# The last gate chunk of a pooling mixer by seven block products too, and five low parts of weights on VectorE

## The chip, the cores and the metric

The kernel runs on one core of a Trainium2 chip. Its metric is the time of one execution on the device in microseconds (us), lower is better. The engines are TensorE (PE in the profile), VectorE (DVE), ScalarE (ACT), GpSimd (POOL) and SyncE (SP, which here issues nearly all the DMAs). Each runs its own instructions strictly in order; they meet only through semaphores.

## What is computed

Two blocks follow each other on a 1024 x 1024 float32 activation. The change touches the first one, and there the part from the input projection to the pooling branch's output projection:

```python
def first_block(x, ...):
    u = rms_norm(h, norm_in_g[l])
    proj = jnp.einsum('bsd,de->bse', u, w_in[l])              # 1024 -> 4096
    pool_x, pool_z, m_x, m_z = jnp.split(proj, [D_POOL, 2 * D_POOL, 2 * D_POOL + D_MLSTM], axis=-1)
    y_pool = pool_mixer(pool_x, pool_w[l], pool_scale[l]) * jax.nn.silu(pool_z)
    y_m = mlstm_branch(m_x, ...) * jax.nn.silu(m_z)
    h = h + jnp.einsum('bse,ed->bsd', jnp.concatenate([y_pool, y_m], axis=-1), w_out[l])

def pool_mixer(u, pool_w, pool_scale):
    ug = u.reshape(B, S, N_POOL_GROUPS, POOL_GROUP_DIM)       # 4 groups of 256
    pooled = stack([window_mean_minus_self(ug[:, :, g], w) for g, w in enumerate((2, 4, 8, 16))])
    mixed = jnp.einsum('bsgc,gcd->bsgd', pooled, pool_w).reshape(B, S, D_POOL)
    return mixed * pool_scale
```

`pool_z` (columns 1024 to 2047 of `w_in`, chunks 4 to 7) is the gate of the pooling branch.

## The kernel before

**Chunks.** Weights come in chunks of 1 MB, in the order of `chunk_plan` (line 90); chunk w of the plan is not the same as the column block c that stands in it. A chunk is loaded into the one buffer `wraw` by SP (`wt`), and split into a high part `whi` and a low part `wlo` (the raw value minus the high part), each in one of two buffers. A product of two float32 matrices is then three matmuls, low x high, high x low and high x high (`three`, lines 1064 to 1066), 128x512 each. In `group` TensorE makes one output tile of 128x512 of a chunk: 8 x 3 matmuls for `w_in`, four such groups in a chunk, or 4 x 3 matmuls for `w_out`, eight groups in a chunk.

**Seven products.** The chunks 2 to 8 of the plan (`SEVEN`, line 104) are computed another way: the chunk is cut into 2 x 2 blocks and the result made of seven block products in place of eight, each 4 x 3 matmuls (`seven`). Sums of blocks are made by GpSimd, their high parts by ScalarE (`cast_block`) and their low parts by VectorE and GpSimd (`low_block`). Each product's weights take one of eight slots, four in each side of `whi` and `wlo` (`place`, `slot`); VectorE adds the products up (`add_up`), and a finished chunk is stored to DRAM from `sz` (`store_7`), except the last, which is the gate of group 0 and stays in `sz`. Chunks 6 to 8 of the plan are gates of the pooling branch; the fourth gate is chunk 12, `W_SZ3`, by four plain groups.

**Behind the products** come, on TensorE: `W_POOL[1]` (chunk 9) with `mix(0)` between its second and third group, `W_POOL[2]` (10) and `mix(1)`, `W_POOL[3]` (11) and `mix(2)`, `W_SZ3` (12), and then `W_OP` (13 to 16), the output projection, with `mix(3)` after its fourth group. `mix(g)` is 4 x 6 matmuls, the pooled features of group g times `pool_w`. VectorE makes the pooled features in `window(g, m)`, their low parts in `low_mix(g)`, and in `mixed(g)` it takes the four results of `mix(g)` out, scales them by the gate `sz` into `yr`, waits for ScalarE's high part `yp_hi` (`high_y`), and makes the low part `yp_lo`. ScalarE's queue at group g is: four copies of a chunk's groups to `px` (`pooled`), `high_pw(g)`, which waits for the end of `mix(g - 1)`, `high_px(g, 0)`, `high_y` for the results of `mix(g - 1)`, `high_px(g, 1)`.

**Splitting a plain chunk.** `split` (line 798) on GpSimd waits for the chunk's load and for TensorE to be done with the chunk two before it, or, where that one went by products, with the last product on its side (`side_free`). It casts the high part (line 804) and, unless the chunk stands in `BY_VECTOR`, makes the low part (line 808). For a chunk in `BY_VECTOR` VectorE makes it in `low_w` (line 1796). TensorE waits for the low part before each group. SP loads chunk w only when `w_lo` has counted w low parts.

**Banks.** PSUM has eight banks of 128x512, named bank0 to bank3 and (as halves) wide0 and wide1. Products take them in turn; plain groups go round bank 0 to 3 (`ring_g`), mixes round the other four (`ring_x`). `take` makes TensorE wait until what a bank last held has been read.

## Time and profile before

| | |
|---|---|
| median of 3 runs | 1151.78 us (1151.3 to 1154.06) |
| profiled execution | 1151.01 us, its span 1149.2 us |
| TensorE busy | 1139.6 us (99%), 6515 matmul records |
| VectorE / ScalarE / GpSimd busy | 724.4 / 386.6 / 477.1 us |
| granted TensorE clock, mean | 0.999 |
| phase of products | about 62 to 196 us of the span |
| chunks 9 to 12 and the mixes | about 196 to 299 us |

Times in rows are in us from the span's start unless marked ns. Matmuls are pipelined: one lasts 0.39 us in the record, while the next starts 0.23 us after it, so the step from start to start tells the pace. "[2.60 <-DMA x]" behind a row is the idle time of the engine before it and what ended it.

### The profile page before, as it was taken

How to read it: one execution, taken by the hardware profiler on the slowest of the kernel's cores; microseconds unless marked ns; L12 is line 12 of the kernel's file. 1: busy time of each engine (PE TensorE's matmuls, PEld its weight loads, DVE VectorE, ACT ScalarE, POOL GpSimd, SP SyncE). 2: the span in 40 equal slices, each digit the busy share in tenths (PEclk: the TensorE clock that was granted, in tenths of full speed). 3: DMA queues.
4: the chain of work that ended last, by engine and by line, in shares of the span. 5: the costliest groups of instructions: out<-in, count | busy, mean ns of one | idle time of the engine just before them, and what ended most of it. 6: DMA issues, size and time to landing. Idle time of an engine off the chain costs nothing.

```text
span 1149.2 us, 17423 instructions
## 1 busy us (share of the span) xinstructions
PE 1139.6 (99%) x6515; PEld 930.8 (81%) x6515; DVE 724.4 (63%) x1336; ACT 386.6 (34%) x758; POOL 477.1 (42%) x474
## 2 busy tenths in 40 slices
PE   9999999999999999999999999999999999999997
PEld 6888888888888887788888888889888887777786
DVE  5944534567244894467777965884698434556668
ACT  7422233222100122546574621341111134553322
POOL 3356654422223231344666765304223224455534
PEclk9999999999999999999999999999999999999999
DMA  8323343222335522101114241232111220142113
GB/s 245 120 64 121 100 146 120 74 65 100 110 73 203 194 85 81 53 23 28 48 42 160 75 165 54 93 125 74 48 45 42 63 72 1 38 154 96 46 39 138
DMA packets 84229, 104.07 MB, mean 91 GB/s; under 512 B 14257, under 2 KB 61577, under 8 KB 82994
## 3 DMA queue, kind: packets, MB, share of 16 engines
q1 hardware_dynamic: 76422, 99.21, 26.0%
q10 hardware_dynamic: 7724, 3.74, 1.2%
q8 instruction: 53, 0.87, 0.3%
q14 instruction: 30, 0.25, 0.1%
HBM read 80.35 MB, written 24.17 MB: 91 GB/s over the span
## 4 chain that ended last, share of the span: by engine, by line
PE 96%; POOL 2%; issue 1%; DVE 1%; ACT 0%; ACTq 0%; POOLq 0%; DVEq 0%
PE bank L1064 22%; PE bank L1066 21%; PE bank L1065 21%; PE bank L1394 3%; PE bank L1369 3%; PE wide L1064 3%; PE wide L1065 3%; PE wide L1066 3%; PE wide L1594 2%; PE wide L1385 2%; PE bank L1333 1%; PE bank L1322 1%; PE bank L1569 1%; PE bank L1310 1%; PE bank L1106 1%
## 5 line engine op out<-in xcount | busy, mean ns | idle before, releaser
L804 POOL CAST whi<-wraw 128x2048 fp32r<-128x2048 f32 x24 | 48.1, 2003 | 336.8 <-PE bank L1066 267.7
L1064 PE MATMUL bank<-x_hi,wlo 128*128 128x512 f32 x312 | 123.5, 396 | 0.0
L1066 PE MATMUL bank<-x_hi,whi 128*128 128x512 f32 x312 | 121.6, 390 | 0.0
L1065 PE MATMUL bank<-x_lo,whi 128*128 128x512 f32 x312 | 121.5, 389 | 0.0
L1064 PE MATMUL bank<-u_hi,wlo 128*128 128x512 f32 x308 | 120.3, 391 | 0.0
L1066 PE MATMUL bank<-u_hi,whi 128*128 128x512 f32 x308 | 119.9, 389 | 0.0
L1065 PE MATMUL bank<-u_lo,whi 128*128 128x512 f32 x308 | 119.9, 389 | 0.0
L808 POOL TENSOR_TENSOR wlo<-wraw,whi 128x2048 fp32r<-128x2048 f32 x20 | 94.8, 4742 | 2.0 <-ACT whi L2909 0.5
L1064 PEld LDWEIGHTS bank<-x_hi,wlo 128*128 128x128 f32 x312 | 58.6, 188 | 16.2 <-issue 4.3
L1008 POOL TENSOR_SCALAR sp<-sp,rcx 128x384 f32<-128x384 f32 (+1 forms) x64 | 37.9, 606 | 76.4 <-DVE rcx L2393 76.3
L2306 DVE SCALAR_TENSOR_TENSOR wide<-glu,VT,wide 128x1024 f32<-128x1024 f32 x58 | 69.3, 1286 | 0.0
L1066 PEld LDWEIGHTS bank<-x_hi,whi 128*128 128x128 f32 x312 | 58.6, 188 | 12.4
L1064 PEld LDWEIGHTS bank<-u_hi,wlo 128*128 128x128 f32 x308 | 57.8, 188 | 13.1 <-issue 1.2
L1065 PEld LDWEIGHTS bank<-x_lo,whi 128*128 128x128 f32 x312 | 58.6, 188 | 11.7
L1066 PEld LDWEIGHTS bank<-u_hi,whi 128*128 128x128 f32 x308 | 57.8, 188 | 12.2
L1065 PEld LDWEIGHTS bank<-u_lo,whi 128*128 128x128 f32 x308 | 57.8, 188 | 11.8
L1394 PE MATMUL bank<-v,kwb 128*128 128x257 f32 x224 | 58.2, 382 | 0.2
L1369 PE MATMUL bank<-Cst,qT 128*128 128x257 f32 x224 | 58.0, 380 | 0.1
L932 POOL TENSOR_TENSOR Pm<-ST,Wb 128x128 f32<-128x128 f32 x64 | 30.0, 470 | 63.0 <-ACT Wb L2784 63.0
L1064 PE MATMUL bank<-whi,ym_lo 128*128 128x512 f32 x128 | 51.2, 400 | 0.0
L1066 PE MATMUL bank<-whi,ym_hi 128*128 128x512 f32 x128 | 49.9, 390 | 0.0
L1065 PE MATMUL bank<-wlo,ym_hi 128*128 128x512 f32 x128 | 49.8, 389 | 0.0
(431 smaller groups left out, 2840.9 us busy)
## 6 DMA issues: line engine op xcount, KB each, us to landing
wraw<-in_w_in SPq DMA_DIRECT2D x19, 1024.0 KB, 5.4
wraw<-in_w_out SPq DMA_DIRECT2D x12, 1024.0 KB, 5.4
wraw<-in_w_in SPq DMA_DIRECT2D x16, 512.0 KB, 4.8
xr<-in_x SPq DMA_DIRECT2D x8, 512.0 KB, 6.9
hst<-in_x SPq DMA_DIRECT2D x4, 1024.0 KB, 5.2
hpool<-hst SPq DMA_DIRECT2D x4, 1024.0 KB, 4.2
h<-hpool SPq DMA_DIRECT2D x4, 1024.0 KB, 7.0
resid<-h SPq DMA_DIRECT2D x8, 512.0 KB, 2.6
```

The costliest lines, as they stand in the source:

```text
L804: g_.tensor_copy(whi[w % 2][:, :, :], wraw[:, :, :]).then_inc(s["w_hi"], 1)
L808: g_.tensor_tensor(wlo[w % 2][:, :, :], wraw[:, :, :], whi[w % 2][:, :, :].bitcast(F32), ALU.subtract).then_inc(s["w_lo"], 1)
L932: g_.tensor_tensor(Pm[:, n % 2, :], STs[h % 2][:, ck, :], Wb[:, n % 2, :], ALU.mult).then_inc(s["g_P"], 1)
L1008: g_.tensor_scalar(row, row, rcx[:, x % 2, i:i + 1], 0.5 if g else 1.0, ALU.mult, ALU.mult).then_inc(s["g_nm"], 1)
L1064: pe.matmul(ps, al, bh, start=(k == 0), stop=False)
L1065: pe.matmul(ps, ah, bl, start=False, stop=False)
L1066: return pe.matmul(ps, ah, bh, start=False, stop=(k == nk - 1))
L1369: mm = pe.matmul(ps[:, 0:AUG], q[:, k, ck * P:(ck + 1) * P], Cst[:, d, k, :], start=(k == 0), stop=(k == 1))
L1385: pe.matmul(ps[:, 0:AUG], Pm[:, n % 2, :], v[:, ck, :], start=True, stop=True).then_inc(s["t_intra"], 1)
L1394: mm = pe.matmul(ps[:, 0:AUG], kwb[:, m % 2, k * P:(k + 1) * P], v[:, ck, :], start=True, stop=True)
L1594: mm = pe.matmul(ps[64 * i:64 * i + 64, 0:P], vt[:, lo + b, g * HD2:(g + 1) * HD2], pT_of(x, i)[:, b * P:(b + 1) * P], start=(b == 0), sto ...
L2306: ins = ve.scalar_tensor_tensor(dst, src, w, acc, ALU.mult, ALU.add)
```

## The change

Column block 7 of `w_in`, the fourth gate, moves from a plain chunk (`W_SZ3`, 12) into the products, which now are chunks 2 to 9 of the plan. `W_POOL[1]` to `W_POOL[3]` become chunks 10, 11 and 12; `W_OP` stays 13. With 56 products instead of 49 the two sides of the buffers come free in the other order, so behind the phase a chunk's buffer is `home(w)` and no longer w % 2. The gate in `sz` at the end of the phase is again that of group 0; the other three are stored and loaded back (`load_sz(1)` to `load_sz(3)`, one more than before). The low parts of the five chunks 10 to 14 are all made by VectorE (`W_POOL[1]` was already); GpSimd only casts there. The first four sums of the output projection are taken out before `mixed(3)`, and its groups all use banks 0 to 3. Where the diff changes `whi[w % 2]` to `whi[home(w)]` in other places, it is cut:

```diff
@@ -90,7 +90,7 @@
-    plan = [("w_in", c, "f") for c in (0, 12, 8, 9, 10, 13, 6, 5, 4, 1, 2, 3, 7)]
+    plan = [("w_in", c, "f") for c in (0, 12, 8, 9, 10, 13, 7, 6, 5, 4, 1, 2, 3)]
     plan += [("w_out_pool", c, "o") for c in (0, 2, 1, 3)]
@@ -101,7 +101,7 @@
-SEVEN = range(2, 9)
+SEVEN = range(2, 10)
@@ -112,12 +112,16 @@
-    W_POOL, W_SZ3, W_OP, W_MX, W_MZ, W_OM, W_2 = (0, 9, 10, 11), 12, 13, 14, 16, 20, 24
+    W_POOL, W_OP, W_MX, W_MZ, W_OM, W_2 = (0, 10, 11, 12), 13, 14, 16, 20, 24
     N7, S0 = len(SEVEN), SEVEN[0]
-    BY_VECTOR = (W_POOL[1], W_MZ + 2, W_MZ + 3, W_OM, W_OM + 1)
+    BY_VECTOR = (W_POOL[1], W_POOL[2], W_POOL[3], W_OP, W_OP + 1, W_MZ + 2, W_MZ + 3, W_OM, W_OM + 1)
     (W_BA, W_BB, W_AV, W_KV, W_Q0, W_AU, W_AG, W_CG0, W_BG, W_CG1, W_Q1) = range(W_2, W_2 + 11)
     W_O2 = W_2 + 11
+
+    def home(w):
+
+        return (w + (w > SEVEN[-1])) % 2
@@ -171,7 +175,7 @@
     um_d = nc.dram_tensor("umraw", [P, 6, S], F32).ap()
-    sz_d = nc.dram_tensor("szpool", [P, 2, 2, S], F32).ap()
+    sz_d = nc.dram_tensor("szpool", [P, 3, 2, S], F32).ap()
     row_t = nc.dram_tensor("relr", [8, RELS], F32)
@@ -375,7 +379,7 @@
         early = {
-            "l_sz": ("l_h0", 32), "l_um0": ("l_h1", 16), "l_um1": ("l_h2", 16), "l_um2": ("l_h3", 16),
+            "l_sz": ("l_h0", 48), "l_um0": ("l_h1", 16), "l_um1": ("l_h2", 16), "l_um2": ("l_h3", 16),
             "o_st0": ("l_kB", 16 * (N7 - 1)), "o_st1": ("l_ln", 16 * (N7 - 1)),
@@ -588,7 +592,7 @@
                 sp_.wait_ge(s["o_st1"], 16 * (N7 - 1))
-                sp_.dma_start(sz[:, :, :], sz_d[:, 2 - g, :, :]).then_inc(s["l_sz"], 16)
+                sp_.dma_start(sz[:, :, :], sz_d[:, 3 - g, :, :]).then_inc(s["l_sz"], 16)
@@ -613,9 +617,8 @@
             mix_weights(2)
-            wt(W_SZ3)
+            wt(W_OP)
             load_sz(2)
-            wt(W_OP)
             sp_.wait_ge(s["v_px"], 13)
@@ -639,6 +642,7 @@
                 load_h(0, q)
+            load_sz(3)
             wt(W_OP + 2)
@@ -798,14 +802,14 @@
                     if w - 2 in SEVEN:
-                        g_.wait_ge(s["t_prod"], side_free(w % 2))
+                        g_.wait_ge(s["t_prod"], side_free(home(w)))
                     elif w >= 2:
                         g_.wait_ge(s["t_gemm"], done(w - 2))
-                    g_.tensor_copy(whi[w % 2][:, :, :], wraw[:, :, :]).then_inc(s["w_hi"], 1)
+                    g_.tensor_copy(whi[home(w)][:, :, :], wraw[:, :, :]).then_inc(s["w_hi"], 1)
                 if w in BY_VECTOR:
                     return
                 g_.wait_ge(s["w_hi"], high_count(w))
-                g_.tensor_tensor(wlo[w % 2][:, :, :], wraw[:, :, :], whi[w % 2][:, :, :].bitcast(F32),
+                g_.tensor_tensor(wlo[home(w)][:, :, :], wraw[:, :, :], whi[home(w)][:, :, :].bitcast(F32),
                                  ALU.subtract).then_inc(s["w_lo"], 1)
@@ -1070,7 +1074,7 @@
                 _, _, layout = plan[w]
-                wh, wl = whi[w % 2], wlo[w % 2]
+                wh, wl = whi[home(w)], wlo[home(w)]
                 nk = KT
@@ -1242,8 +1246,6 @@
                 mix(g - 1)
-            for i in range(4):
-                group(W_SZ3, i, u_hi, u_lo, "a_sz", 8 + i + 1)
             pool_hi = lambda j: yp_hi[:, j, :]
@@ -1255,7 +1257,7 @@
                     group(W_OP + q, i, pool_hi, pool_lo, "v_hp", n,
-                          ps=ring_x("v_hp", n) if q == 0 and i >= 4 else None)
+                          ps=None)
@@ -1808,10 +1810,10 @@
-                if g in (1, 2):
+                if g:
                     ve.wait_ge(s["l_sz"], 16 * g)
                 else:
-                    ve.wait_ge(s["a_sz"], 8 + 4 * (g == 3))
+                    ve.wait_ge(s["a_sz"], 10)
                 for i in range(5):
@@ -1877,13 +1879,33 @@
             window(1, 0)
+            low_w(W_POOL[2])
             window(1, 1)
             low_mix(1)
-            for g in (2, 3):
-                window(g, 0)
-                mixed(g - 1)
-                window(g, 1)
-                low_mix(g)
+            window(2, 0)
+            mixed(1)
+            low_w(W_POOL[3])
+            window(2, 1)
+            low_mix(2)
+            low_w(W_OP)
+            for m in range(2):
+                window(3, m)
+            low_mix(3)
+            mixed(2)
+
+            def empty_out(n):
+
+                q, t = n // NT, n % NT
+                if q % 2:
+                    ve.wait_ge(s["v_hp"], n - 7)
+                else:
+                    ve.wait_ge(s[f"l_xh{t // 4}"], 16 * (q // 2 + 1))
+                ps = filled(ve, "t_gemm", first[W_OP + q] + t + 1, "v_hp", n + 1)
+                ve.tensor_tensor(hst[:, t, :], ps[:, :], hst[:, t, :], ALU.add).then_inc(s["v_hp"], 1)
+
+            for n in range(4):
+                empty_out(n)
+            low_w(W_OP + 1)
             mixed(3)
@@ -1954,12 +1976,8 @@
                             fold_keys(t - 6)
-                    if q % 2:
-                        ve.wait_ge(s["v_hp"], n - 7)
-                    else:
-                        ve.wait_ge(s[f"l_xh{t // 4}"], 16 * (q // 2 + 1))
-                    ps = filled(ve, "t_gemm", first[W_OP + q] + t + 1, "v_hp", n + 1)
-                    ve.tensor_tensor(hst[:, t, :], ps[:, :], hst[:, t, :], ALU.add).then_inc(s["v_hp"], 1)
+                    if n >= 4:
+                        empty_out(n)
                     if n >= 26:
@@ -2684,15 +2702,12 @@
                 high_px(g, 0)
+                if g == 3:
+                    high_px(g, 1)
                 for n in range(4 * g - 4, 4 * g):
                     high_y(n)
-                if g == 3:
-                    ac.wait_ge(s["v_yr"], 12)
-                    for i in range(4):
-                        m, nh = i // 2, i % 2
-                        ps = filled(ac, "t_gemm", first[W_SZ3] + i + 1, "a_sz", 8 + i + 1)
-                        ac.activation(sz[:, m, nh * HALF:(nh + 1) * HALF], ps[:, :], ACT.Silu).then_inc(s["a_sz"], 1)
-                high_px(g, 1)
+                if g < 3:
+                    high_px(g, 1)
             for n in range(12, 16):
```

VectorE at the end of the products, the last chunk's additions (`t_cv` is the count of products, `v_ug` that of the additions, `g_gob` that of GpSimd's blocks). Before:

```order
L1770 TENSOR_TENSOR sz<-bank3,yr 128x512 [waits v_ug,t_cv]
L1796 TENSOR_TENSOR wlo1<-wraw,whi1 128x2048 [waits w_hi,g_gob]
L1802 TENSOR_TENSOR pwlo<-pw,pwhi 128x512 [waits a_mixhi]
L1806 TENSOR_TENSOR yp_lo<-px,yp_hi 128x1024 [waits a_mixhi] x2
L1770 TENSOR_TENSOR yr<-wide0,yr 128x512 [waits v_ug,t_cv]
L1770 TENSOR_TENSOR sz<-bank1,yr 128x512 [waits v_ug,t_cv,l_ln]
L1770 TENSOR_TENSOR sz<-wide0,yr 128x512 [waits v_ug,t_cv]
```

After:

```order
L1772 TENSOR_TENSOR sz<-bank2,yr 128x512 [waits v_ug,t_cv]
L1798 TENSOR_TENSOR wlo1<-wraw,whi1 128x2048 [waits w_hi,g_gob]
L1804 TENSOR_TENSOR pwlo<-pw,pwhi 128x512 [waits a_mixhi]
L1808 TENSOR_TENSOR yp_lo<-px,yp_hi 128x1024 [waits a_mixhi] x2
L1772 TENSOR_TENSOR yr<-bank3,yr 128x512 [waits v_ug,t_cv]
L1772 TENSOR_TENSOR sz<-bank0,yr 128x512 [waits v_ug,t_cv,l_ln]
L1772 TENSOR_TENSOR sz<-wide0,yr 128x512 [waits v_ug,t_cv]
```

The order is the same; what moved is the banks: the last addition but one reads bank 0, not bank 1. TensorE's first plain group behind the products writes bank 0 in both kernels.

VectorE from `mixed(1)` on, behind `mix(1)`. Before (the window follows at once, and the low part of the next chunk is in GpSimd's queue):

```order
L1829 TENSOR_TENSOR yp_lo<-yr,yp_hi 128x512 [waits a_yhi]
L1829 TENSOR_TENSOR yp_lo<-yr,yp_hi 128x512 [waits a_yhi,v_ylo]
L1783 TENSOR_TENSOR pta<-px 128x1055 [waits a_px,v_ylo]
L1783 TENSOR_TENSOR ptb<-pta 128x1053 [waits v_chain]
L1783 TENSOR_TENSOR pta<-ptb 128x1049 [waits v_chain]
```

After:

```order
L1831 TENSOR_TENSOR yp_lo<-yr,yp_hi 128x512 [waits a_yhi]
L1831 TENSOR_TENSOR yp_lo<-yr,yp_hi 128x512 [waits a_yhi,v_ylo]
L1798 TENSOR_TENSOR wlo1<-wraw,whi1 128x2048 [waits w_hi,v_ylo]
L1785 TENSOR_TENSOR pta<-px 128x1055 [waits a_px]
L1785 TENSOR_TENSOR ptb<-pta 128x1053 [waits v_chain]
```

The low part of `W_POOL[3]` now stands between the last `yp_lo` of `mixed(1)` and `window(2, 1)`. On TensorE, the end of `mix(1)` and the chunk behind it, after:

```order
L1070 MATMUL wide1<-yp_hi,pwhi 128x512
L1068 MATMUL wide0<-yp_hi,pwlo 128x512 [waits v_yr]
L1069 MATMUL wide0<-yp_lo,pwhi 128x512
L1070 MATMUL wide0<-yp_hi,pwhi 128x512
L1068 MATMUL wide0<-yp_hi,pwlo 128x512
L1069 MATMUL wide0<-yp_lo,pwhi 128x512
L1070 MATMUL wide0<-yp_hi,pwhi 128x512
L1068 MATMUL bank0<-u_hi,wlo1 128x512 [waits a_px,w_lo]
```

This part of TensorE's queue is as before: the next chunk's first matmul, which waits for the low part (`w_lo`), stands right behind the mix.

## Rows read from the trace of the kernel before

**Rows 1.** The page, chain that ended last: shares by engine.
```profile
PE 96%; POOL 2%; issue 1%; DVE 1%; ACT 0%; ACTq 0%; POOLq 0%; DVEq 0%
```

**Rows 2.** TensorE's waits: releaser, us in total, times, longest us.
```profile
PE bank L1106 <- POOL eps L813: 1.0, 1, 1.0
PE bank L1310 <- issue: 0.8, 1, 0.8
...
```

**Rows 3.** Busy us (instructions) of each engine in a stretch, clock, DMA share, GB/s.
```profile
60.00:240.00 180.00, 180.00 (x795) 148.81 (x794) 89.75 (x107) 50.94 (x81) 92.32 (x59) 1.00 0.34 107
```

**Rows 4.** Timeline of TensorE: start, us, engine, line, operation, out<-in.
```profile
73.38 0.47 PE L1064 MATMUL bank<-u_hi,wlo 128*128 128x512 f32 x1
...
190.43 0.39 PE L1064 MATMUL wide<-Thi,wlo 128*128 128x512 f32 x1
...
195.87 0.39 PE L1064 MATMUL bank<-u_hi,wlo 128*128 128x512 f32 x1
...
244.83 0.39 PE L1064 MATMUL wide<-yp_hi,pwlo 128*128 128x512 f32 x1
...
250.27 0.39 PE L1064 MATMUL bank<-u_hi,wlo 128*128 128x512 f32 x1
```

**Rows 5.** Timeline of GpSimd, product blocks and casts of plain chunks.
```profile
71.95 1.29 POOL L845 TENSOR_TENSOR wlo<-xsum,whi 128x512 fp32r<-128x512 f32 x1 [0.81 <-ACT whi L2589]
...
182.89 1.74 POOL L845 TENSOR_TENSOR wlo<-wraw,whi 128x512 fp32r<-128x512 f32 x1
190.92 1.90 POOL L804 CAST whi<-wraw 128x2048 fp32r<-128x2048 f32 x1 [6.29 <-DMA wraw<-in_w_in]
...
245.13 1.90 POOL L804 CAST whi<-wraw 128x2048 fp32r<-128x2048 f32 x1 [14.30 <-PE bank L1066]
```

**Rows 6.** Timeline of SP, the load of the chunk behind the products.
```profile
184.66 0.38 SPq L508 DMA_DIRECT2D wraw<-in_w_in  x1
```

**Rows 7.** Timeline of VectorE, end of the products to window(1, 0).
```profile
192.91 2.29 DVE L1796 TENSOR_TENSOR wlo<-wraw,whi 128x2048 fp32r<-128x2048 f32 x1 [1.59 <-POOL whi L804]
...
198.82 0.69 DVE L1770 TENSOR_TENSOR sz<-bank,yr 128x512 f32<-128x512 f32 x1
...
208.39 0.75 DVE L1821 SCALAR_TENSOR_TENSOR yr<-wide,VT,sz 128x512 f32<-128x512 f32 x1 [8.29 <-PE wide L1066]
...
213.99 0.69 DVE L1829 TENSOR_TENSOR yp_lo<-yr,yp_hi 128x512 fp32r<-128x512 f32 x1 [0.17 <-ACT yp_hi L2640]
...
217.70 1.23 DVE L1789 SCALAR_TENSOR_TENSOR px<-ptb,px 128x1024 f32<-128x1024 f32 x1
```

**Rows 8.** Timeline of VectorE, mixed(1): its first row, its wait, its last.
```profile
246.57 0.75 DVE L1821 SCALAR_TENSOR_TENSOR yr<-wide,VT,sz 128x512 f32<-128x512 f32 x1 [3.30 <-PE wide L1066]
...
252.66 0.69 DVE L1829 TENSOR_TENSOR yp_lo<-yr,yp_hi 128x512 fp32r<-128x512 f32 x1 [4.16 <-ACT yp_hi L2640]
...
256.30 0.69 DVE L1829 TENSOR_TENSOR yp_lo<-yr,yp_hi 128x512 fp32r<-128x512 f32 x1 [0.17 <-ACT yp_hi L2640]
```

**Rows 9.** Timeline of ScalarE, high_pw(2) behind mix(1).
```profile
250.53 0.63 ACT L2625 ACTIVATE pwhi<-pw 128x512 fp32r<-128x512 f32 x1 [4.90 <-PE wide L1066]
```

**Rows 10.** Timeline of VectorE, first addition of window(3, 0), nothing beside it.
```profile
266.68 1.26 DVE L1783 TENSOR_TENSOR pta<-px 128x1055 f32<-128x1055 f32 x1 [1.15 <-ACT px L2557]
```

**Rows 11.** Timeline of VectorE, an addition of window(1, 1), beside GpSimd's low part.
```profile
226.41 5.54 DVE L1783 TENSOR_TENSOR ptb<-pta 128x1053 f32<-128x1053 f32 x1
```

**Rows 12.** Stretches at the end of the span; the clock follows the POOL column.
```profile
1142.00:1143.00 1.00, 0.57 (x6) 0.42 (x4) 0.82 (x3) 0.00 (x0) 1.00 (x1) 1.00 0.00 0
...
1145.00:1146.00 1.00, 0.00 (x0) 0.00 (x0) 0.97 (x2) 0.00 (x0) 0.00 (x0) 1.00 0.50 201
1146.00:1147.00 1.00, 0.00 (x0) 0.00 (x0) 0.75 (x1) 0.00 (x0) 0.00 (x0) 0.51 0.70 262
```

**Rows 13.** Timeline of TensorE at the program start, one microsecond each.
```profile
4.39 1.92 PE L1106 MATMUL bank<-ones 128*128 128x384 f32 x3
...
5.67 1.29 PE L1106 MATMUL bank<-ones 128*128 128x384 f32 x3
```

More of the change, by code:

```diff
@@ L244, in slot_free, with side_free @@
             return ("t_gemm", 4 + 4 * (place(b) // 4)) if b < 8 else ("t_prod", b - 7)
-        def side_free(side):
-            return max(b for b in range(7 * N7) if place(b) // 4 == side) + 1
+        def side_free(q):
+            return max(b for b in range(7 * N7) if place(b) // 4 == q) + 1
         def raw(f, k):
@@ L988, in split_part @@
                 ks = slice(2 * part, 2 * part + 2)
-                g_.tensor_copy(whi[w % 2][:, ks, :], wraw[:, ks, :]).then_inc(s["g_part"], 1)
+                g_.tensor_copy(whi[home(w)][:, ks, :], wraw[:, ks, :]).then_inc(s["g_part"], 1)
                 parts[0] += 1
                 g_.wait_ge(s["g_part"], parts[0])
-                ins = g_.tensor_tensor(wlo[w % 2][:, ks, :], wraw[:, ks, :], whi[w % 2][:, ks, :].bitcast(F32),
+                ins = g_.tensor_tensor(wlo[home(w)][:, ks, :], wraw[:, ks, :], whi[home(w)][:, ks, :].bitcast(F32),
                                        ALU.subtract)
@@ L1478, in _ @@
             c, t = slice(mt * P, (mt + 1) * P), slice(nh * HALF, (nh + 1) * HALF)
-            wh, wl = whi[W_BA % 2], wlo[W_BA % 2]
+            wh, wl = whi[home(W_BA)], wlo[home(W_BA)]
             for k in range(KT + 1):
@@ L1795, in low_w @@
                 ve.wait_ge(s["w_hi"], high_count(w))
-                ve.tensor_tensor(wlo[w % 2][:, :, :], wraw[:, :, :], whi[w % 2][:, :, :].bitcast(F32),
+                ve.tensor_tensor(wlo[home(w)][:, :, :], wraw[:, :, :], whi[home(w)][:, :, :].bitcast(F32),
                                  ALU.subtract).then_inc(s["w_lo"], 1)
@@ L2271, in _ @@
             ve.wait_ge(s["w_hi"], high_count(W_BB))
-            ve.tensor_tensor(wlo[W_BB % 2][:, :, :], wraw[:, :, :], whi[W_BB % 2][:, :, :].bitcast(F32), ALU.subtract
+            ve.tensor_tensor(wlo[home(W_BB)][:, :, :], wraw[:, :, :], whi[home(W_BB)][:, :, :].bitcast(F32), ALU.subtract
                              ).then_inc(s["w_lo"], 1)
@@ L2908, in high_w @@
                 ac.wait_ge(s["t_gemm"], done(w - 2))
-                ac.activation(whi[w % 2][:, :, :], wraw[:, :, :], ACT.Copy).then_inc(s["w_hi"], 1)
+                ac.activation(whi[home(w)][:, :, :], wraw[:, :, :], ACT.Copy).then_inc(s["w_hi"], 1)
             for t in range(4):
```

## The prediction

> **What bounds the kernel now.** I read the page's chain of work first: it is 96% TensorE [rows 1]. Then the table of waits for TensorE alone: it idled in four places, 1.0 us at the very start and at most 0.8 us elsewhere [rows 2]. Idle time shorter than a matmul's own 0.39 us is hidden in such a table, so I checked the pace: 795 matmuls in the 180 us from 60 to 240 us is one per 0.2264 us [rows 3], and in the timeline 24 matmuls (two products) take the 5.44 us from 190.43 to 195.87, as 24 of a mix take from 244.83 to 250.27, one per 0.2266 [rows 4]. TensorE is the bound, and it doesn't wait in the stretch that the change touches. Each matmul removed gives 0.2266 us back, and each wait added is added to the end in full: no idle time is left behind it that could take it up.
>
> **Products, and what they save.** A direct chunk of the input projection is 4 groups of 8 x 3 = 96 matmuls; a chunk by seven products is 7 x 4 x 3 = 84. The last gate chunk changes from one to the other: 12 x 0.2266 = **2.72 us less**. Both kinds run at the same cadence, so nothing else is gained.
>
> **The weights around the products: hidden.** GpSimd ends the last block of the last chunk at 182.89 + 1.74 = 184.63 [rows 5]. It takes no more than TensorE's 7 x 2.72 = 19.03 us a chunk, so an eighth is ready by 203.7; its sixth product, which needs that block, starts at 190.43 + 19.03 = 209.5. SP then issues the next weights at once, as at 184.66 [rows 6], and GpSimd's cast gets them 6.3 us later, at 190.92 now [rows 5]: 208.7 to 210.0 in the new kernel, the earlier if GpSimd keeps its lead of each chunk (17.7 us by the ends of the last two, 19.03 at worst). The cast also needs its side of the buffers free. That is now the end of the last chunk's fifth product, 209.46, with 0.30 for the lag between TensorE's 244.83 and GpSimd's 245.13 [rows 4, 5]: 209.76. Taken back by the 19.03 us of the extra chunk this is 190.73, against 190.92 now. Cast 1.90, low part 2.29 [rows 5, 7]: ready by 195.1, and TensorE wants it at 195.87. Hidden, by 0.7 us.
>
> **The first new wait: bank 0.** The products go round all eight banks. With 49 of them the last chunk had its third product in bank 1, and the first direct group behind the phase took bank 0, long free. With 56 the third product lies in bank 0. VectorE frees it with its last addition but one, which stands in its queue behind the low part, `pwlo`, two `yp_lo` and another addition. From row to row that is 192.91 to 198.82 + 0.69 = 199.51 [rows 7]; 0.19 earlier, as the cast is: 199.32. A semaphore to TensorE takes 0.14 (GpSimd's 71.95 + 1.29 = 73.24, TensorE's 73.38) [rows 4, 5]. TensorE wants bank 0 at 195.87: 199.46 - 195.87 = **3.6 us more**. Bounds: 3.3 without the lag of 0.30, and 4.9 if the weights land at 210.0 and one more lag comes on top.
>
> **The low part behind window(1, 0): hidden.** In the old kernel this window ends at 217.70 + 1.23 = 218.93 [rows 7]; a low part behind it ends at 221.3, and TensorE wants it at 223.1 (195.87 and 120 matmuls). Both count from the same start of TensorE's, so the first wait leaves this 1.7 us as it is.
>
> **The second new wait: the low part behind mixed(1).** This is the big one. TensorE runs the four groups of `W_POOL[2]`, mix(1) from 244.83 to 250.27, and then `W_POOL[3]` [rows 4]. Its low part was GpSimd's, made under the groups; before its cast at 245.13 GpSimd had idled 14.3 us [rows 5]. Now it stands on VectorE behind mixed(1), which works on what mix(1) has just produced. Mixed(1) begins at 246.57, waits 4.16 us at 252.66 for ScalarE, whose `pwhi` waits until mix(1) is over (250.53), and ends at 256.30 + 0.69 = 256.99 [rows 8, 9]. Add 0.03 between instructions, 2.29 for the low part and 0.14 for the semaphore: 259.45, where TensorE wants it at 250.27. **9.2 us more.** Lower bound 5.1: mixed(0), which ScalarE didn't hold up, took 213.99 + 0.69 - 208.39 = 6.29 [rows 7], so 246.57 + 6.29 + 2.29 + 0.14 = 255.3. Upper bound 11.1, with one GpSimd cast of 1.90 in its way. I take the middle value, since it is this very mixed(1) that was measured. Queued behind it are, on VectorE, window(2, 1) and low_mix(2), and on SP the weights of `W_OP`, which wait for this low part; all have the 27 us of `W_POOL[3]` and mix(2).
>
> **The other moved low parts: hidden.** Counted from the start of `W_POOL[3]` (T): the weights of `W_OP`, issued at T, need 6.3 + 1.9 + 2.3, so its low part is made by T + 11. window(3, 1), whose first addition is 1.26, needs four of those, two of 0.2 and a last of 1.3 [rows 10], 6.8 us; it waits for the fourth group's copy at T + 22.7, so it ends at T + 29.5, and low_mix(3) at T + 32.6. TensorE's mix(3) wants that at T + 38.1 (168 matmuls). Mixed(2), four additions, the low part of `W_OP` + 1 and mixed(3) follow in a row: 6.3 + 2.8 + 2.3 + 6.3 = 17.7, up to T + 50.3. TensorE's second output chunk wants the last `yp_lo` at T + 54.4. This cover of 4 us is the thinnest in this part, since SP now loads the last gates behind two loads of 1 MB. Behind this place both kernels do the same work with the buffers swapped.
>
> **What the move gives back: nothing.** GpSimd's subtraction holds VectorE up: beside one, a window's addition took 5.54 us at 226.41, against 1.26 at 266.68 [rows 10, 11]. But VectorE isn't late there. The Trainium skill ("SBUF — State Buffer", section "Who interferes with whom") says that a VectorE instruction with two SBUF inputs and a GpSimd instruction that reads SBUF exclude each other. By that rule, with which the row agrees, GpSimd's subtractions are worth removing; it adds nothing to the sum, for the place on VectorE is what costs.
>
> **The clock.** TensorE's last matmul ends within the slice 1142 to 1143 (0.57 us of it busy); its granted clock is 1.00 up to 1146 and 0.51 from 1146 to 1147, half of full speed (1.2 against 2.4 GHz) [rows 12]. The second wait, 9.2 us, is longer than the 3.4 us of idle time in front of that fall. What half speed costs is seen at the start of the program: three matmuls span 1.92 us from 4.39, and three of the same shape span 1.29 from 5.67 [rows 13]: with 0.64 for the last one's own length, the two steps are 0.64 us each and then 0.32. From the first matmul, at 1.0, to 5.67 is 4.6 us at half pace, which costs half of itself: **2.3 us more**, behind the second wait; bounds 0 and twice that. The first wait of 3.6 us is about as long as that idle time; I take no loss there and keep 2.3 for the range. The Trainium skill ("TensorE: Matmul & The Clock Gate", section "HAM oscillation — how this bites in real kernels") describes a kernel whose waits for data return the array to half rate again and again. It speaks against this change: by it the second wait is paid for twice, as rows 12 bear out, and if it did not hold the sum would be 2.3 lower.
>
> **The sum.** -2.72 + 3.6 + 9.2 + 2.3 = +12.4 us. The profiled execution took 1151.01 (a span of 1149.2 and 1.8 around it), so 1163.4; the median of the runs is 0.77 higher, which gives **1164.2**.
>
> **The rivals.**
> 1. The clock stays up: 1164.2 - 2.3 = 1161.9. Against it, the fall at the end of this trace. Chance 0.11.
> 2. The clock is lost at both waits, or twice as long at one: 1166.5. For it, the first wait is as long as the idle time before that fall. Chance 0.14.
> 3. The thin cover of mixed(3) breaks because the gates land 6 or 7 us late: +2 to 3, 1167. Chance 0.06.
> 4. Only one wait is real. Without the second the clock isn't lost either: 1151.8 - 2.7 + 3.6 = 1152.7, chance 0.04. Without the first: 1160.6, chance 0.04.
> 5. Not slower: TensorE runs through and only the 12 matmuls show, 1151.8 - 2.7 = 1149.1. The place that decides is the first matmul of `W_POOL[3]`, and its price is 9.2 + 2.3. The wait is gone if mixed(1) is over by 250.27 - 2.29 - 0.14 = 247.8, 1.3 us behind its first step, while its inputs take TensorE until 250.27; so it takes another instruction that brings the count of low parts to 13, which I don't find. That the change doesn't do what it says is the same case. Chance 0.03.
> The forecast itself has 0.58.
>
> **How the numbers follow.** A measurement of this kernel can tell about 0.3%, 3.5 us, from no change. Even 1149.1 is within that, so faster gets 0.01; same has that case and the one at 1152.7, 0.07; slower 0.92. The low end is the second wait halfway to its lower bound with no loss of clock, 1161.9 - 2.1 = 1159.8, rounded down to 1159.5, which takes in the case at 1160.6. The high end is rival 2 with the upper bound of the first wait, 1166.5 + 1.3, rounded up to 1168. Left out are 1152.7, 1149.1 and the far ends of the others.
>
> **What would show it.** In the new trace: 12 fewer matmuls; a wait of TensorE of 3 to 4 us near 215, ended by VectorE's `sz<-bank`; one of about 9 us near 273, ended by VectorE's `wlo`; a granted clock of 0.5 in the slices behind it; no third wait of a microsecond up to 400. A wait near 215 of over 5 us would say that the cast or its weights are late, not the bank. If the wait near 273 is absent, the forecast is wrong.

## The result, and the profile after

The kernel after takes 1164.12 us (median of 4 runs, 1162.67 to 1164.76), the kernel before beside it 1151.65 (1151.3 to 1154.06). The ratio is 1.0103, with a 95% interval of 1.009 to 1.0116: it is slower, by 12.5 us, where the prediction said 12.4. The profiled execution took 1164.76, its span is 1163.0 us; that is 13.8 us longer than the span before.

The page of after, busy time and instructions of each engine, then the chain that ended last:

```profile
PE 1139.9 (98%) x6503; PEld 930.2 (80%) x6503; DVE 738.5 (63%) x1350; ACT 392.0 (34%) x764; POOL 461.1 (40%) x476
...
PE 95%; DVE 2%; POOL 1%; issue 1%; ACT 0%; DMA 0%; ACTq 0%; DVEq 0%; POOLq 0%
```

There are 12 matmul records fewer (6503 against 6515), yet TensorE's busy time did not fall (1139.6 before): some matmuls ran longer. Against [rows 1] VectorE came into the chain, with 2%.

TensorE's waits after, in us: releaser, total, times, longest:

```profile
PE bank L1068 <- DVE wlo L1798: 8.9, 1, 8.9
PE bank L1068 <- DVE sz L1772: 3.5, 1, 3.5
PE bank L1110 <- POOL eps L817: 1.0, 1, 1.0
PE wide L1121 <- DMA hot<-in_hot: 1.0, 1, 1.0
PE bank L1312 <- issue: 0.8, 1, 0.8
```

Where [rows 2] had nothing above 1.0 us there are two waits, each on the operation that the prediction named. (The 1.0 us for `hot` is at 7 us, in the program's start; there TensorE goes on at 7.18, and at 7.04 in the kernel before.) Both waits in TensorE's timeline (start, us, line, operation):

```profile
214.88 0.39 PE L1070 MATMUL wide<-Thi,whi 128*128 128x512 f32 x1
218.73 0.47 PE L1068 MATMUL bank<-u_hi,wlo 128*128 128x512 f32 x1 [3.46 <-DVE sz L1772]
219.04 0.58 PE L1069 MATMUL bank<-u_lo,whi 128*128 128x512 f32 x1
219.42 0.63 PE L1070 MATMUL bank<-u_hi,whi 128*128 128x512 f32 x1
219.85 0.63 PE L1068 MATMUL bank<-u_hi,wlo 128*128 128x512 f32 x1
...
274.64 0.39 PE L1070 MATMUL wide<-yp_hi,pwhi 128*128 128x512 f32 x1
283.96 0.79 PE L1068 MATMUL bank<-u_hi,wlo 128*128 128x512 f32 x1 [8.93 <-DVE wlo L1798]
284.55 0.63 PE L1069 MATMUL bank<-u_lo,whi 128*128 128x512 f32 x1
```

The next matmul was due one step of 0.23 us after the last: at 215.11 and at 274.87. The waits cost 218.73 - 215.11 = 3.62 us and 283.96 - 274.87 = 9.09 us. Behind each of them the step from matmul to matmul is 0.43 us in place of 0.2266 [rows 4] for a while. What held the first one stands in VectorE's timeline:

```profile
212.00 2.29 DVE L1798 TENSOR_TENSOR wlo<-wraw,whi 128x2048 fp32r<-128x2048 f32 x1 [1.43 <-POOL whi L808]
214.21 0.69 DVE L1804 TENSOR_TENSOR pwlo<-pw,pwhi 128x512 fp32r<-128x512 f32 x1
214.81 2.36 DVE L1808 TENSOR_TENSOR yp_lo<-px,yp_hi 128x1024 fp32r<-128x1024 f32 x2
217.08 0.68 DVE L1772 TENSOR_TENSOR yr<-bank,yr 128x512 f32<-128x512 f32 x1
217.90 0.69 DVE L1772 TENSOR_TENSOR sz<-bank,yr 128x512 f32<-128x512 f32 x1
```

These are the same instructions in the same order as in [rows 7], and the addition that frees bank 0 is the last one shown: 217.90 + 0.69 = 218.59, and TensorE goes on 0.14 later. The second wait, VectorE again:

```profile
271.17 0.75 DVE L1823 SCALAR_TENSOR_TENSOR yr<-wide,VT,sz 128x512 f32<-128x512 f32 x1 [6.28 <-PE wide L1070]
...
277.26 0.69 DVE L1831 TENSOR_TENSOR yp_lo<-yr,yp_hi 128x512 fp32r<-128x512 f32 x1 [4.15 <-ACT yp_hi L2658]
...
280.89 0.69 DVE L1831 TENSOR_TENSOR yp_lo<-yr,yp_hi 128x512 fp32r<-128x512 f32 x1 [0.17 <-ACT yp_hi L2658]
281.61 2.29 DVE L1798 TENSOR_TENSOR wlo<-wraw,whi 128x2048 fp32r<-128x2048 f32 x1
```

Mixed(1) runs as in [rows 8], with the same 4 us of waiting for ScalarE (4.15 against 4.16), and the low part stands behind its last step. TensorE has had nothing to do since 274.87.

The clock, in stretches of one microsecond (columns as in [rows 3]; the clock follows the POOL column). The first four are at the first wait, the next two within the second and the last two behind it:

```profile
218.00:219.00 1.00, 0.27 (x1) 0.30 (x2) 1.00 (x2) 0.00 (x0) 0.00 (x0) 1.00 1.08 377
219.00:220.00 1.00, 1.00 (x4) 0.77 (x3) 0.18 (x1) 0.78 (x1) 0.33 (x1) 0.54 0.66 219
...
222.00:223.00 1.00, 1.00 (x5) 0.81 (x4) 0.00 (x0) 0.00 (x0) 0.00 (x0) 0.75 0.00 0
223.00:224.00 1.00, 1.00 (x6) 0.83 (x5) 0.00 (x0) 0.00 (x0) 0.00 (x0) 1.00 0.00 0
276.00:277.00 1.00, 0.00 (x0) 0.00 (x0) 0.00 (x0) 1.00 (x2) 0.00 (x0) 1.00 0.00 0
277.00:278.00 1.00, 0.00 (x0) 0.00 (x0) 0.71 (x2) 0.74 (x2) 0.00 (x0) 0.55 0.00 0
...
287.00:288.00 1.00, 1.00 (x5) 0.77 (x5) 0.93 (x3) 0.00 (x0) 0.00 (x0) 0.83 1.06 414
288.00:289.00 1.00, 1.00 (x6) 0.82 (x5) 0.97 (x2) 0.00 (x0) 0.00 (x0) 1.00 1.09 440
```

The grant went to half at both places. At the second it fell during the wait, about 2.1 us after TensorE's last matmul had ended, and came back 3.4 us behind the restart. At the first it was still 1.00 in the slice in which TensorE started again, and fell only then. By the starts of the matmuls, the first 24 behind the first wait took 7.18 us where 24 x 0.2266 is 5.44, and the first 18 behind the second 5.82 where 4.08 was due: 1.74 us lost at each.

In this execution the sum is -2.72 + 3.62 + 1.74 + 9.09 + 1.74 = 13.5 of the 13.8 us; 0.14 of the rest is the later start at 7 us.

### The profile page after: what moved, and what is told of

It is laid out like the page before. It is cut to its first block, busy times and chain, and to the rows that moved or that the text cites. A ratio compares the mean times of both kernels' runs of the same rounds, so it can differ in the third digit from the quotient of the medians.

```text
span 1163.0 us, 17447 instructions
## 1 busy us (share of the span) xinstructions
PE 1139.9 (98%) x6503; PEld 930.2 (80%) x6503; DVE 738.5 (63%) x1350; ACT 392.0 (34%) x764; POOL 461.1 (40%) x476
## 4 chain that ended last, share of the span: by engine, by line
PE 95%; DVE 2%; POOL 1%; issue 1%; ACT 0%; DMA 0%; ACTq 0%; DVEq 0%; POOLq 0%
PE bank L1068 22%; PE bank L1070 21%; PE bank L1069 21%; PE bank L1371 3%; PE bank L1396 3%; PE wide L1070 3%; PE wide L1069 3%; PE wide L1068 3%; PE wide L1387 2%; PE wide L1596 2%; PE bank L1335 1%; PE bank L1324 1%; PE bank L1312 1%; PE bank L1571 1%; PE wide L1571 1%
## 5 line engine op out<-in xcount | busy, mean ns | idle before, releaser
L808 POOL CAST whi<-wraw 128x2048 fp32r<-128x2048 f32 x23 | 45.2, 1966 | 360.9 <-PE bank L1070 252.2
L1068 PE MATMUL bank<-u_hi,wlo 128*128 128x512 f32 x280 | 110.9, 396 | 12.4 <-DVE wlo L1798 8.9
L1069 PE MATMUL bank<-u_lo,whi 128*128 128x512 f32 x280 | 110.3, 394 | 0.0
L1070 PE MATMUL bank<-u_hi,whi 128*128 128x512 f32 x280 | 110.2, 394 | 0.0
L1068 PEld LDWEIGHTS bank<-u_hi,wlo 128*128 128x128 f32 x280 | 53.4, 191 | 25.5 <-DVE wlo L1798 9.3
L812 POOL TENSOR_TENSOR wlo<-wraw,whi 128x2048 fp32r<-128x2048 f32 x15 | 70.1, 4675 | 1.6 <-ACT whi L2924 0.5
L1070 PEld LDWEIGHTS bank<-x_hi,whi 128*128 128x128 f32 x312 | 58.6, 188 | 12.5
L1070 PEld LDWEIGHTS bank<-u_hi,whi 128*128 128x128 f32 x280 | 53.4, 191 | 11.3
L1069 PEld LDWEIGHTS bank<-u_lo,whi 128*128 128x128 f32 x280 | 53.3, 191 | 11.1
L1744 DVE TENSOR_TENSOR wlo<-wraw,whi 128x512 fp32r<-128x512 f32 x24 | 17.4, 755 | 52.6 <-ACT whi L2607 52.6
```

Of the source, the lines that this page charges most:

```text
L808: g_.tensor_copy(whi[home(w)][:, :, :], wraw[:, :, :]).then_inc(s["w_hi"], 1)
L812: g_.tensor_tensor(wlo[home(w)][:, :, :], wraw[:, :, :], whi[home(w)][:, :, :].bitcast(F32), ALU.subtract).then_inc(s["w_lo"], 1)
L1068: pe.matmul(ps, al, bh, start=(k == 0), stop=False)
L1069: pe.matmul(ps, ah, bl, start=False, stop=False)
L1070: return pe.matmul(ps, ah, bh, start=False, stop=(k == nk - 1))
```

## Experiments

The theory: the time is made of two waits, each from the place of one VectorE instruction in its queue, and of the clock that they cost. The rivals: the waits are hidden by something else once one of them is gone; the cost is in the products or in the order of VectorE's work as a whole; the low parts on VectorE cost or bring something by themselves.

### One wait at a time

e1_low_before_mixed, from the kernel after:

```diff
             window(2, 0)
-            mixed(1)
             low_w(W_POOL[3])
+            mixed(1)
             window(2, 1)
```

> The changed kernel with one line moved: VectorE makes the low part of W_POOL[3] in front of mixed(1), not behind it. The two-waits theory (each new wait of TensorE stands on its own and is followed by a stretch at half clock): the wait of 9.1 us near 275 us and its slow matmuls are gone, the one of 3.6 us near 215 us stays, so 1164.1 - 9.1 - 1.7 = 1153.3 us, 1152 to 1154.5 by whether the first wait loses the clock. The rival (the low part is late because its weights or its cast are late): a wait of several us before W_POOL[3] stays, over 1156 us.

Measured: 1154.01 us (1153.57 to 1155.29, 9 runs), ratio to before 1.0023 (1.0013 to 1.0033), within the expected range. The wait of 8.9 us is gone and the one of 3.5 is left.

e2_bank_turn, from the kernel after: the products begin one bank further on, so that the last but one addition no longer holds bank 0:

```diff
-            turn = [5]
+            turn = [6]
```

> The changed kernel with one number changed: the products start one bank later, so that the last chunk's third product lies in bank 1 and not in bank 0, as before the change. The bank theory: the wait of 3.6 us near 215 us and the stretch at half clock behind it are gone, the wait of 9.1 us stays: 1164.1 - 3.6 - 1.7 = 1158.8 us (1158.5 to 1160.5, as the clock was not lost there in every run). The rival (TensorE waits there for the low part of W_POOL[1], made in the last two products' time): the wait stays and the time is 1164 us.

Measured: 1160.68 us (1159.95 to 1161.44, 4 runs), ratio 1.0079 (1.0065 to 1.0093), just above the expected range. Only the wait of 8.9 us is left.

e3_both, both edits:

> The changed kernel with both edits, the low part in front of mixed(1) and the products one bank later. The two-waits theory: nothing is left but the 12 matmuls fewer, 1151.65 - 2.72 = 1148.9 us, a ratio of 0.9976 to before. The rival (part of the loss is spread thinly, in collisions of VectorE and GpSimd or in the third gate load): 1150.5 us or more.

Measured: **1148.52 us** (1148.08 to 1149.29, 8 runs), ratio 0.9974 (0.9964 to 0.9984). TensorE's waits in e3_both, and its row for the 240 us around both places:

```profile
PE bank L1110 <- POOL eps L817: 1.0, 1, 1.0
PE bank L1312 <- issue: 0.8, 1, 0.8
PE wide L1387 <- POOL Pm L936: 0.3, 1, 0.3
...
60.00:300.00 240.00, 240.00 (x1060) 198.48 (x1059) 130.73 (x152) 67.33 (x105) 96.47 (x67) 1.00 0.31 99
```

TensorE starts 1060 matmuls in 240 us, one per 0.2264, as in [rows 3]: it doesn't wait. The gain on before, 1151.35 beside it, is 1151.35 - 1148.52 = 2.83 us, and 12 x 0.2266 is 2.72. So the seven products bring what was reckoned, and the two instructions take it back more than five times over. Nothing else in the change leaves a wait in TensorE's table; by the interval of the ratio (1.8 to 4.1 us gained) a further cost of up to 1 us could not be told. From 1148.52 the first wait costs 1154.01 - 1148.52 = 5.5 us and the second 12.2, where the idle time alone is 3.6 and 9.1. The rest, 1.9 and 3.1 us, is most of it the clock: by the starts of the matmuls in the traces, the 24 steps behind the restart lost 1.50 us in e1 and 2.95 us in e2. Fillers test it below.

### The same two costs in the kernel before

If place alone makes a wait, the kernel before must get it too, without an eighth chunk and with most low parts left on GpSimd. e4_before_bank, from the kernel before:

```diff
-            turn = [5]
+            turn = [4]
```

> The kernel before with the products started one bank earlier, so that the last chunk's third product lies in bank 0, and nothing else changed. The bank theory: a wait of 3.8 us at 195.9 us (199.51 + 0.14 - 195.87), with or without a stretch at half clock: 1151.65 + 3.8 = 1155.5 us, or 1157.2 with the clock. The rival (the wait comes of the eighth chunk and its weights): no change, 1151.7 us.

Measured: 1157.9 us (1156.59 to 1160.19, 4 runs), ratio 1.0057 (1.0043 to 1.0071); more than either expected value, and with a wider spread than the other kernels' runs. The wait is there, and in the profiled execution it is longer. TensorE's wait, then GpSimd's cast, VectorE's low part and the addition that frees the bank:

```profile
PE bank L1064 <- DVE sz L1770: 5.4, 1, 5.4
...
193.08 1.90 POOL L804 CAST whi<-wraw 128x2048 fp32r<-128x2048 f32 x1 [6.70 <-DMA wraw<-in_w_in]
...
195.08 2.29 DVE L1796 TENSOR_TENSOR wlo<-wraw,whi 128x2048 fp32r<-128x2048 f32 x1 [3.35 <-POOL whi L804]
...
200.97 0.69 DVE L1770 TENSOR_TENSOR sz<-bank,yr 128x512 f32<-128x512 f32 x1
```

The wait ends as reckoned with the addition that reads the bank, but everything in front of it hangs on the weights, for which the cast here waited 2.2 us longer than in [rows 5] (it starts at 193.08 against 190.92). The load was not slow: GpSimd ended its last block at 186.38 in place of 184.63, and SP issued the load at 186.41 in place of 184.66 [rows 6], so 1.75 of the 2.2 us were there before it. Why GpSimd was later is not shown. The cover of 0.7 us in front of the low part is more than used up, and the wait is longer for it. In the kernel after the cast began at 210.00, close to the 209.8 reckoned, and what ended its wait was TensorE's product, not the load. So the size of such a wait depends on what else is late in front of it.

e7_before_low_late, from the kernel before: only the low part of `W_POOL[3]` goes to VectorE behind mixed(1).

```diff
-    BY_VECTOR = (W_POOL[1], W_MZ + 2, W_MZ + 3, W_OM, W_OM + 1)
+    BY_VECTOR = (W_POOL[1], W_POOL[3], W_MZ + 2, W_MZ + 3, W_OM, W_OM + 1)
...
                 mixed(g - 1)
+                if g == 2:
+                    low_w(W_POOL[3])
                 window(g, 1)
```

> The kernel before with one low part moved, that of W_POOL[3], from GpSimd to VectorE behind mixed(1); products as before. The theory: a wait of 9.2 us at 250.3 us and 1.7 us of slow matmuls behind it, 1151.4 + 10.9 = 1162.2 us. The rival (the wait needs the eighth chunk, its swapped buffers or the late weights): under 1155 us.

Measured: 1164.15 us (1163.1 to 1166.13, 4 runs), ratio 1.0118 (1.0101 to 1.0135); 2 us more than the 1162.2 expected. TensorE waits 8.9 us for `wlo`: its matmuls start at 250.39 and then at 259.71. The wait is as reckoned; what was too small is the clock behind it, 1.7 us expected and 2.58 lost by the starts of the next 24 matmuls. One instruction behind mixed(1) gives the whole second wait; the other chunks' low parts have no share in it.

### The clock by itself

If the remainder is the clock, the same waits must cost only their idle time when TensorE works through them. e5_fillers, from the kernel after, puts matmuls of ones into both waits, 5 and 13 (each shows as two rows in the trace); the groups behind overwrite their banks:

```diff
+            fill_wait(take(5, *last[5]), 5)
...
+                    if g == 3 and i == 0:
+                        ps = ring_g("a_px", 13)
+                        fill_wait(ps, 13)
+                        group(W_POOL[g], i, u_hi, u_lo, "a_px", 13, ps=ps)
+                        continue
                     group(W_POOL[g], i, u_hi, u_lo, "a_px", 4 * g + i + 1)
```

> The changed kernel, with matmuls of ones on TensorE placed in its two new waits: five of 128x384 into bank 5 in front of W_POOL[1], thirteen into the free bank of the first group of W_POOL[3]; their results are overwritten. Each takes 0.64 us, so 3.2 and 8.3 us, both shorter than the waits of 3.6 and 9.1. If half clock behind a wait follows from TensorE's idleness, the granted clock stays 1.00 at both places and the waits stay as long: 1164.1 - 2 x 1.7 = 1160.7 us (1160.3 to 1161.5). The rival (the slow matmuls come of something else there, a load or the buffers): 1164.1 us and a clock of 0.5 as before, or more if the fillers outlast the waits.

Measured: 1161.83 us (1161.27 to 1162.29, 4 runs), ratio 1.0092 (1.0077 to 1.0107); 0.3 us above the expected range. Stretches around the two places:

```profile
214.00:224.00 10.00, 9.76 (x39) 7.06 (x38) 4.83 (x7) 1.06 (x1) 1.90 (x1) 1.00 0.43 131
274.00:290.00 16.00, 15.46 (x59) 10.70 (x58) 14.13 (x15) 4.20 (x6) 2.06 (x1) 1.00 0.37 131
```

The clock stays at 1.00, and the span is 1159.5: 1149.2 - 2.72 + 3.62 + 9.09 = 1159.2. The medians say that the clock cost the kernel after 1164.12 - 1161.83 = 2.3 us, but the intervals of the two ratios overlap, so this number is loose; the two profiled spans say 3.5, which is what the starts of the matmuls give (1.74 twice).

e10_low_late_fillers is e7 with the same 13 matmuls in its wait:

> The kernel of e7 (before, one low part behind mixed(1)) with thirteen matmuls of ones, 8.3 us, in TensorE's wait of 9.2 us. If all that e7 lost beyond its wait was clock: 1151.3 + 9.2 = 1160.5 us, 3.6 below e7, with a granted clock of 1.00 all through. The rival (part of e7's loss is elsewhere, in later waits): 1162 us or more, with a wait of TensorE behind 260 us that the table shows.

Measured: 1160.49 us (1160.07 to 1160.7, 4 runs), ratio 1.0075 (1.0058 to 1.0092). The clock is 1.00 from 249 to 265. Against e7's 1164.15 that is 3.7 us for the clock behind one wait (3.0 by the two spans), and here the intervals of the ratios lie apart. So a loss of clock at such a wait is shown; its size is not one number (below).

### What the low parts on VectorE bring

The prediction said that taking the subtractions from GpSimd gives nothing back. e6_gpsimd_lows is e3_both with four of them back on GpSimd, in the new order:

```diff
-    BY_VECTOR = (W_POOL[1], W_POOL[2], W_POOL[3], W_OP, W_OP + 1, W_MZ + 2, W_MZ + 3, W_OM, W_OM + 1)
+    BY_VECTOR = (W_POOL[1], W_MZ + 2, W_MZ + 3, W_OM, W_OM + 1)
...
-            low_w(W_POOL[2])
...
-            low_w(W_POOL[3])
...
-            low_w(W_OP)
...
-            low_w(W_OP + 1)
```

> The kernel of e3 with the four low parts of W_POOL[2], W_POOL[3], W_OP and W_OP + 1 back on GpSimd, so of the change only the eighth products' chunk and the third gate load remain. If moving the low parts to VectorE is worth nothing: the same as e3, 1148.5 us, with VectorE's additions held up to 5 us again where nobody waits. The rival (GpSimd's subtractions hold VectorE up so that TensorE waits): over 1150 us and a wait of TensorE between 220 and 340 us.

Measured: 1151.94 us (1150.45 to 1152.62, 10 runs), ratio 1.0003 (0.9994 to 1.0012): 3.4 us more than e3_both. TensorE's waits, VectorE's addition in window(3, 1), GpSimd's low part beside it, and the loaded gates' first use:

```profile
PE wide L1068 <- DVE yr L1823: 1.5, 1, 1.5
...
PE bank L1068 <- DVE hst L1901: 0.9, 1, 0.9
...
295.21 5.56 DVE L1785 TENSOR_TENSOR ptb<-pta 128x1053 f32<-128x1053 f32 x1
...
294.15 5.51 POOL L812 TENSOR_TENSOR wlo<-wraw,whi 128x2048 fp32r<-128x2048 f32 x1
...
319.99 1.41 DVE L1823 SCALAR_TENSOR_TENSOR yr<-wide,VT,sz 128x512 f32<-128x512 f32 x2 [3.79 <-DMA sz<-szpool]
```

The addition lasts as long as GpSimd's subtraction, 5.56 us in place of 1.25, as in [rows 11]. Mixed(2) begins at 307.92 where it began at 304.89 in e3_both; mix(3) finds its bank unread at 306.97 and waits 1.5 us. SP issues the last gates' load only when mixed(2) has read `sz` for the last time, so it goes 3.0 us later too (312.25 against 309.22), mixed(3) waits 3.8 us for it, and a bank of the output projection comes free 0.9 us late. The two waits of TensorE cost 1.6 and 1.1 us from start to start, 2.7 of the 2.9 us between the two spans. The Trainium skill ("SBUF — State Buffer", section "Who interferes with whom") says that a VectorE instruction with two SBUF inputs contends with a GpSimd instruction that reads SBUF, and that the port pair they share is an exclusive lock. This row agrees: the addition ends 1.1 us after GpSimd's subtraction does, and here, unlike in the prediction, the rule changes the time.

How thin the cover at this place is shows in e3_both, by VectorE's last step of mixed(3), the addition behind it and the matmul of TensorE that needs both (240 steps behind the start of `W_POOL[3]`):

```profile
322.01 0.69 DVE L1831 TENSOR_TENSOR yp_lo<-yr,yp_hi 128x512 fp32r<-128x512 f32 x1 [0.17 <-ACT yp_hi L2658]
322.74 2.48 DVE L1904 TENSOR_TENSOR hst<-bank,hst 128x512 f32<-128x512 f32 x4
...
323.77 0.39 PE L1068 MATMUL bank<-whi,yp_lo 128*128 128x512 f32 x1
```


e9_old_order asks whether the new order in which VectorE, ScalarE and the banks work is needed for the seven products' gain. It is e6 with the order of before: mixed(2) ahead of window(3, 1), groups 4 to 7 of `W_OP` in the mixes' banks, the gates loaded earlier.

```diff
+            for g in (2, 3):
+                window(g, 0)
+                mixed(g - 1)
+                window(g, 1)
+                low_mix(g)
```

> The eighth products' chunk with the products one bank later, low parts on GpSimd as before the change, and also VectorE's, ScalarE's and the banks' order of before (mixed(2) in front of window(3, 1), the output groups 4 to 7 in the mixes' banks). The reading that the new order belongs to the chunk's removal: TensorE reaches mix(3) 21.75 us earlier than it did, at T + 38.1 from the start of W_POOL[3], while the old order has low_mix(3) ready near T + 44 (before: 294.2 - 250.3), so it waits about 6 us, with a loss of clock behind it: 1148.5 + 6 + 2 = 1156.5 us, over 1154. The rival (the new order is only there for the moved low parts, and the 3.4 us that e6 lost against e3 come of it): 1148.5 to 1150 us.

Measured: 1156.22 us (1156.01 to 1156.76, 4 runs), ratio 1.0038 (1.0023 to 1.0053).

```profile
PE wide L1068 <- DVE yp_lo L1808: 5.5, 1, 5.5
```

With no plain gate chunk ahead of it, mix(3) comes 96 x 0.2266 = 21.8 us earlier in TensorE's queue, and the old order delivers its features 5.5 us late. So the new order as a whole is needed (tried with the low parts on GpSimd only, and its pieces not one by one), and in it the low parts on VectorE are worth 3.4 us; only two places are wrong.

### The first wait another way

e8_adds_first keeps the banks and, with e1's edit, puts `low_mix(0)` behind the additions that free bank 0:

```diff
                     low_w(W_POOL[1])
-                    low_mix(0)
                 add_up(c, 4)
...
+                else:
+                    low_mix(0)
                 add_up(c, 6)
```

> The kernel of e1 (first wait only) with VectorE's additions that read banks 3 and 0 put in front of low_mix(0), behind the low part of W_POOL[1]. The bank theory, with VectorE's queue as the cause: bank 0 is free at 214.3 + 1.5 = 215.8 us and TensorE waits 0.9 us instead of 3.6, without a loss of clock: 1154.0 - 2.7 - 1.7 = 1149.6 us (1149.4 to 1150.5). The rival (any use of bank 0 there costs the whole wait): 1154.0 us.

Measured: 1149.67 us (1148.94 to 1151.98, 10 runs), ratio 0.9987 (0.9978 to 0.9996). Waits and clock:

```profile
PE bank L1068 <- DVE sz L1772: 0.7, 1, 0.7
...
214.00:220.00 6.00, 5.30 (x24) 4.10 (x23) 5.42 (x7) 0.41 (x1) 0.00 (x0) 1.00 0.69 215
```

Taking the 3.0 us of `pwlo` and `yp_lo` out of the way leaves a wait of 0.7 us that loses no clock; it is 1.2 us behind e3_both, where the bank isn't needed at all.

## Why the prediction was right, and where it was not

- **The products**: 2.7 us predicted; 12 records fewer, and 2.8 us by e3_both.
- **The weights around the products**: hidden as said. The cast began at 210.00 (209.76 reckoned) and the low part was ready at 214.29, 0.8 us ahead of 215.11. e4 shows that such a cover doesn't hold in every kernel of this shape.
- **The first wait**: 3.6 predicted, 3.62 measured, on the instruction named. The sum was copied row by row from the same place in the kernel before, and only the bank's number was new. Its upper bound, 4.9, does not follow from the terms named: a cast at 210.0 and one more lag of 0.30 give 4.1. That moves only the top of the range, from 1168 to 1167.
- **The second wait**: 9.2 predicted, 9.09 measured. Choosing the middle value was right: mixed(1) repeated its 4.15 us of waiting for ScalarE, which is set by TensorE's own mix. The difference is the step to TensorE, 0.06 us here against the 0.14 taken.
- **The other low parts**: hidden, and so was mixed(3). Its gates ended a wait of VectorE of 1.3 us at 331.02, as feared of a load behind two others, but it was over by 336.79 and TensorE did not wait. There is no third wait of a microsecond behind the start. The cover of 4 us was reckoned too high, though: in e3_both, without the two waits, the last `yp_lo` was ready 1.1 us and the bank 0.3 us ahead of TensorE. The sum had left out VectorE's wait for the gates (1.55 us there) and that the bank is read only behind mixed(3).
- **The clock**: here steps failed. "I take no loss there", said of the first wait, is wrong: 1.74 us were lost at it in the profiled execution, and e1 shows the slow stretch with that wait alone. The wait had been compared with the 3.4 us of idle time in [rows 12], which it exceeds by 0.2, and the prediction still took the favorable side. The idle time before the fall was 2.1 to 4.7 us at the waits of these kernels (table below), so the 3.4 was one case and no limit. The 2.3 us behind the second wait were 1.74 in that execution: the start of the program, from which it was taken, ran slow for 4.6 us and this restart for 3.4; in e2, at the same wait, it was 6.0 and 2.95 were lost. Nor does the record of the clock bear out the source of the 2.3: from 1 to 5 us of that trace it shows 1.00, where the matmuls go at half pace. That this pace is a half clock was argued from the steps of [rows 13]. The two errors pull in opposite directions. In the profiled execution the clock cost 3.5, which is the mechanism of rival 2 ("The clock is lost at both waits"), though with 1.2 us more than the forecast's and not 2.3. By the medians of e5 it cost 2.3 in all, loosely. That the number of the forecast was met to 0.1 us is partly luck: the two profiled executions, from which the sum was built, lie 13.75 us apart (1151.01 and 1164.76) where 12.4 was said, and only the medians 12.5.
- **"What the move gives back: nothing"** was wrong as an account of the change. It was argued from the kernel before, where VectorE wasn't late. In the new order there is no plain gate chunk ahead of mix(3), and VectorE is just on time: with the subtractions on GpSimd it works 3 us later and TensorE waits (e6). The sum was not hurt by it, because it started from the kernel before and added what is in the new one; but someone who acted on that sentence and kept the low parts on GpSimd would have got 1151.9 in place of 1148.5.

The Trainium skill ("TensorE: Matmul & The Clock Gate", section "HAM oscillation — how this bites in real kernels") tells of a kernel that pays for each wait a second time by restarting at half rate. The two slow stretches behind the waits agree, and e5 and e10 give the price by taking it away.

## What to carry to other kernels

When products or groups go round a ring of banks and their number changes, follow the ring to the first group behind them and see which instruction reads that bank last, and what stands ahead of it in its queue. Before an instruction is moved to another engine, compare its deadline with the inputs of what it stands behind: here one subtraction, due when the mix ended, stood behind work that needed the mix's own end, and moving it one call earlier was worth 10 us. A change that is slower as a whole can hold a faster kernel: take its waits away one by one before it is dropped.
